# Prompt attention in one decoder layer: probabilities turned and multiplied with the values one or two steps behind their logits

## The reference

```python
logits = einsum(q, k) * 64 ** -0.5          # two maps m = 0, 1 per head, width 64 each
bias   = rel_bias[t5_bucket(q_pos - k_pos)] # depends on the distance alone
p      = softmax(where(dist >= 0, logits + bias, -1e30))
attn   = p[:, :, 0] - lam * p[:, :, 1]
out    = einsum(attn, v)                    # then RMSNorm over the 128 columns of a head
```

## Time and profile before

| what | value |
|---|---|
| median of three runs | 1768.83 us (1766.42 to 1769.52) |
| the profiled execution's own time | 1766.95 us |
| its span | 1765.1 us |
| TensorE busy in the span | 1553.6 us |
| mean granted clock of TensorE | 0.94 |
| the prompt's attention | about 484 to 908 us of the span |

### The profile page before, as it was taken

The page is one execution under the profiler, slowest core; times in us unless marked ns, Lnnn a source line. Parts: engine busy times, 40 slices in busy tenths (PEclk is TensorE's granted clock), DMA queues, the critical chain, the costliest instruction groups (busy, mean ns, idle before and its releaser), DMA issues. The chain is left out here.

```text
span 1765.1 us, 22053 instructions
## 1 busy us (share of the span) xinstructions
PE 1553.6 (88%) x7497; PEld 1061.8 (60%) x7498; DVE 707.0 (40%) x1465; ACT 461.4 (26%) x1040; POOL 232.3 (13%) x417
## 2 busy tenths in 40 slices
PE   5999889977499899898879999999889937999996
PEld 3555556555356565555558888888768733444442
DVE  4356877666524444454542221233242251212220
ACT  2223333322123333333432121122132210111110
POOL 1000101010122221222210000000000001222221
PEclk8999999988789998999979999999989968999998
DMA  7000300000030202000034766523253383988973
GB/s 246 16 1 17 116 2 26 1 2 25 26 114 1 62 1 62 1 26 1 1 121 135 249 205 204 168 72 110 84 158 108 108 288 105 317 247 231 297 215 48
DMA packets 119369, 186.03 MB, mean 105 GB/s; under 512 B 9507, under 2 KB 82262, under 8 KB 117222
## 3 DMA queue, kind: packets, MB, share of 16 engines
q1 hardware_dynamic: 107750, 134.41, 24.0%
q0 software_dynamic: 11520, 50.34, 9.8%
HBM read 154.38 MB, written 30.34 MB: 105 GB/s over the span
## 5 line engine op out<-in xcount | busy, mean ns | idle before, releaser
L964 PE MATMUL psum<-attention_part,kept 128*128 128x384 f32 (+1 forms) x576 | 201.0, 504 | 0.8 <-DVE attention_part L1197 0.7
L2158 PE MATMUL psum<-moe_part,kept 128*128 x384 | 172.4, 603 | 6.4 <-issue 4.9
L964 PEld LDWEIGHTS psum<-attention_part,kept 128*128 128x128 f32 (+1 forms) x576 | 108.0, 192 | 76.1 <-issue 16.5
L1430 PE MATMUL psum<-split 128*128 128x368 f32 x384 | 140.6, 366 | 2.5 <-DVE split L1576 2.5
L498 PE MATMUL psum<-kept,recurrence_part 128*128 128x368 f32 x384 | 124.4, 480 | 10.0 <-PEq L236 5.0
L1419 PE MATMUL psum<-kept,sample_part 128*128 128x368 f32 x384 | 131.8, 487 | 1.3 <-PEq L865 1.3
L503 PE MATMUL psum<-recurrence_part,kept 128*128 128x512 f32 (+1 forms) x288 | 126.5, 594 | 1.3 <-DVE kept L684 1.3
L1432 PE MATMUL psum<-split 128*128 128x368 f32 x384 | 127.3, 332 | 0.0
L1431 PE MATMUL psum<-split 128*128 128x368 f32 x384 | 127.0, 331 | 0.0
L2158 PEld LDWEIGHTS psum<-moe_part,kept 128*128 128x128 f32 x384 | 72.3, 193 | 89.7 <-issue 89.7
L518 PE MATMUL psum<-recurrence_part 128*128 128x128 f32 (+1 forms) x480 | 70.8, 308 | 48.9 <-DVE recurrence_part L767 39.4
(11 more groups left out here) (312 smaller groups left out, 2519.6 us busy)
## 6 DMA issues: line engine op xcount, KB each, us to landing
sample_part<-merge_gates POOLq DMA_DIRECT2D x16, 1024.0 KB
merge_part<-cache_kT SPq DMA_DIRECT2D x64, 256.0 KB, 3.3
merge_part<-cache_v SPq DMA_DIRECT2D x64, 256.0 KB, 3.0
moe_part<-w_gate SPq DMA_DIRECT2D x16, 1024.0 KB, 6.1
moe_part<-w_up SPq DMA_DIRECT2D x16, 1024.0 KB, 12.5
moe_part<-w_down SPq DMA_DIRECT2D x16, 1024.0 KB, 14.1
recurrence_part<-w_in SPq DMA_DIRECT2D x8, 1024.0 KB, 8.2
sample_part<-merge_out POOLq DMA_DIRECT2D x16, 512.0 KB, 6.5
```

Source lines behind the costliest of these rows:

```text
L964: mm = pe.matmul(bank_of(("z", h, i))[:ROWS[i], 0:384], K["xT"][:, k, cols(i)], Wb[h % 2][:, k, :], start=(k == 0), stop=(k == KC - 1))
L1430: pe.matmul(bank_of(u, 2 * j + 1), wh[w % 2][:, k, ch], xh[b][:, k, :], start=(k == 0), stop=False)
L2158: mm = pe.matmul(psum[:, 2 + par, :], XT[par][:, k, :], K["GU"][:, bass.ds(KC * b + k, 1), :], start=(k == 0), stop=(k == KC - 1))
```

## The change

The turned probabilities and their product with the values are put two steps behind the logits: slot s turns `Am` of step s - 2 and multiplies it; g of step s - 3 follows. There are 39 slots in place of 38. `Am` gets a second buffer, used by odd and even steps in turn, and `combine(s)` waits for the turning of step s - 2 in place of s - 1. `aT`, `Pm`, the banks and the place of z, L and x stay.

```diff
--- before.py
+++ after.py
@@ -844,17 +844,17 @@
     for n in range(1, AHEAD):
         zx += [make[n], place[n - 1]]
     slots = []
-    for s in range(STEPS + 2):
+    for s in range(STEPS + 3):
         slot = make[s + AHEAD:s + AHEAD + 1]
-        if 1 <= s <= STEPS:
-            slot += [("a", s - 1, g) for g in range(groups(s - 1))]
+        if 2 <= s <= STEPS + 1:
+            slot += [("a", s - 2, g) for g in range(groups(s - 2))]
         if s < STEPS:
             slot += [("L", s, 0), ("L", s, 1)] + ([("e", s, 0)] if s % NQ == NQ - 1 else [])
-        if 1 <= s <= STEPS:
-            slot += [("o", s - 1, 0)]
+        if 2 <= s <= STEPS + 1:
+            slot += [("o", s - 2, 0)]
         slot += place[s + AHEAD - 1:s + AHEAD]
-        if s >= 2:
-            slot += [("g", s - 2, 0)]
+        if s >= 3:
+            slot += [("g", s - 3, 0)]
         slots.append(slot)
     jobs = zx + [j for slot in slots for j in slot if j[0] != "L"]
     turn_of = {j: n for n, j in enumerate(jobs)}
@@ -883,7 +883,7 @@
         Bn = [sb(256) for _ in range(HEADS)]
         rel, rel31, relh, bucket, vecs = sb(HEADS), sb(HEADS), sb(HEADS, P), sb(ND), sb(HEADS, ND)
         Pm = sb(2, SEQ + META)
-        Am, aT = sb(SEQ + META), sb(NT, P)
+        Am, aT = sb(2, SEQ + META), sb(NT, P)
         nmax, sums, coef, ssq, rr, mt = sb(STEPS, 4), sb(STEPS, 4), sb(STEPS, 4), sb(STEPS), sb(STEPS, 2), sb(2, META)
         junk, og = sb(P), sb(2, P)
         block = st.enter_context(nc.Block())
@@ -1006,7 +1006,7 @@
                 bank_free(pe, ("a", s, g))
                 for n in range(4 * g, min(4 * g + 4, i + 1)):
                     w = META if n == i else P
-                    mm = pe.transpose(bank_of(("a", s, g))[:w, P * (n % 4):P * (n % 4) + r], Am[:r, P * n:P * n + w], K["ident"][:r, :r])
+                    mm = pe.transpose(bank_of(("a", s, g))[:w, P * (n % 4):P * (n % 4) + r], Am[:r, s % 2, P * n:P * n + w], K["ident"][:r, :r])
                 mm.then_inc(a_turned, 1)
 
             def outputs(s):
@@ -1241,9 +1241,9 @@
                 dve.drain()
                 dve.tensor_scalar(coef[:r, s, 0:1], sums[:r, s, 0:1], coef[:r, s, 3:4], K["lam"][:r, 3:4], ALU.mult, ALU.mult)
                 dve.drain()
-                if s:
-                    dve.wait_ge(a_turned, a_index[("a", s - 1, groups(s - 1) - 1)] + 1)
-                dve.scalar_tensor_tensor(Am[:r, 0:n], Pm[:r, 1, 0:n], coef[:r, s, 0:1], Pm[:r, 0, 0:n],
+                if s >= 2:
+                    dve.wait_ge(a_turned, a_index[("a", s - 2, groups(s - 2) - 1)] + 1)
+                dve.scalar_tensor_tensor(Am[:r, s % 2, 0:n], Pm[:r, 1, 0:n], coef[:r, s, 0:1], Pm[:r, 0, 0:n],
                                          ALU.mult, ALU.add).then_inc(a_done, 1)
 
             def scale_out(s):
@@ -1284,8 +1284,8 @@
                         normalise(a, b)
                 if s < STEPS:
                     combine(s)
-                if 1 <= s <= STEPS:
-                    scale_out(s - 1)
+                if 2 <= s <= STEPS + 1:
+                    scale_out(s - 2)
 
 
 def load_merge_weights(e, A, K, n):
```

## The result

The changed kernel takes 1.0055 times the time of the kernel before (95% interval 1.0037 to 1.0073): 1779.61 us as the median of 11 runs against 1769.69. By the ratio that is about 9.7 us more. The forecast was 3.9 us more, so the direction held and the size did not. The profiled execution has a span of 1775.1 us at a mean clock of 0.937.

The account below looks back on a forecast made before the run. It took TensorE as the bound, with 45 us idle in the attention. Terms -2.6 - 1.8 - 3.9 + 6.9 + 5.3 = +3.9 us on the 1768.8 median gave 1772.7; own range 1770 to 1776, chance 0.55.

Parts of the forecast that it names:

- The start: Slot 1: turning and o of step 0 leave it, 2.6 us gained, and the next z regains 1.8 us of clock.
- 0 as the other end: Slot 1's next z: 1.8 us gained at full clock, or 0 if the clock is not regained.
- Inside the heads: Tiles 2 to 8 of each head: shorter turning ahead of L, 3.9 us gained over all slots.
- the 0.12 and 0.2: Inside a head: 0.12 us gained per slot by one block less turned, 0.2 us in each tile-5 slot.
- These slots are held by the chain L, maxima, L1197: Tiles 2 to 8: the chain, then x or g, sets slot length, so only the shorter turning gains, 0.12 us a block.
- The changes of head: First two slots of heads 2 to 4: tile-0 gains 1.3 us, tile-1 is 3.6 longer; 2.3 net, three times, +6.9.
- D: Rival: the clock falls at each change of head, slower still; +11.1 us, 1779.9; chance 0.12.
- The drain: Slots 34 to 36: o(34) waits for VectorE's copy and delays o(35); costs 5.3 us.
- rival B: Drain: its o run at full clock, 3.4 us come back, no change; +0.5 us, 1769.3; chance 0.25.
- The prediction's C: Slots 34 to 36: waits for `combine` go, L(34) begins straight behind the turning; -7.7 us, 1761.1; chance 0.08.
- the interior would give nothing: Inside the heads: by the skill's rule a second `Am` alone is the wrong buffer, no gain, where the forecast counts 3.9.

Follow-up runs that it names:

- e_heads: Against the kernel before: two steps behind in the middle only, step 0 and steps 28 to 35 one step behind; ratio 1.0066.
- c_bank: Changed kernel with o(tile 7) and o(tile 8) of the first three heads in PSUM banks 1 and 3; ratio 0.9979 against the kernel before.
- c_fill: Changed kernel with two idle matmuls in the wait ahead of o(34); ratio 1.0035 against the kernel before.
- a_buffer: Kernel before with the second Am buffer alone, in the old order; ratio 1.0008 against the kernel before.
- e_start: Against the kernel before: step 0 alone two steps behind, all others one step behind; ratio 1.0006.
- e_drain: Against the kernel before: one step behind up to step 27, two steps behind from step 28; ratio 1.0030.
- b_between: Kernel before with VectorE's normalise between the two maxima, not behind both; ratio 0.9963 against the kernel before.
- c_between: Changed kernel with normalise between the two maxima; ratio 0.9959 against the kernel before.
- b_bank: Kernel before with o(tile 8) of the first three heads in PSUM bank 1; ratio 0.9963 against the kernel before.
- b_bank_between: b_bank with normalise between the two maxima; ratio 0.9931 against the kernel before.
- c_bank_between: c_bank with normalise between the two maxima; ratio 0.9920 against the kernel before.
- c_bank_between_fill: c_bank_between with the two idle matmuls ahead of o(34); ratio 0.9909 against the kernel before, 1752.46 us.

## Why the prediction came out wrong in size

The sum was +3.9 and the traces have +8.9. The terms that failed are the lower clock at the changes of head, which the forecast took as nothing more than before, and the lower clock of the logits in the drain.

*The start* held: -5.3 for -4.5. The z of slot 2 ran at full clock, which I had taken with 0 as the other end, and slot 2 itself was shorter.

*Inside the heads* -2.4 came for the -3.0 of these slots. The tile-5 slot got shorter by 0.32 to 0.33 us in each of the four heads, which is the 0.12 and 0.2 that I gave it, and those of tiles 6 and 7 by 0.05 to 0.14. Tiles 3 and 4 didn't follow: from 0.45 us shorter to 0.19 longer. "These slots are held by the chain L, maxima, L1197" is wrong for tile 2 as well. In the second head it took 3.58 us from the turning to the next z (624.00 to 627.58) after and 3.53 before (623.08 to 626.61 in the trace of before), although a block less was turned; in the third head 3.44 and 3.91. What holds these short slots isn't settled.

*The changes of head*: forecast +6.9 (+6.2 as the stretches are cut), found +9.1. The waits came where they were put. At the first change the tile-0 slot without its slow z would be 9.8 us for 11.2, a gain of 1.4 where I had 1.3; the tile-1 slot without its slow o is 11.6 for 8.56, 3.0 for the 3.6. That is a cost of 1.6 where I had 2.3, and 1.5 and 1.4 at the other two. The step that failed is the one by which I gave D 0.12 and put its cost into the sum as nothing: that the clock would fall no more than before, because the idle time in these slots would be no more than before. It was no more, and yet the clock fell at all three changes, twice each: o(tile 6) 0.9 to 1.0 us, z 2.0 to 2.1 and o(tile 8) 1.4 to 1.6 over their times at full clock, about 4.5 a head, 13.7 in all. The measured +9.7 is nearer to D's +11.1 than to the forecast. D's own account was short too. It found 3.6 us of such falls in the trace of before, which has about 1.8, 5.5 and 1.2, 8.5 in all. So the clock cost 5.2 us here that the sum lacked, and the waits came 2.3 us cheaper than forecast, which hid half of it: that the total of this term is off by only 2.9 is luck. Part of the 5.2 is the draw of one trace of before; by the means of several traces (e_heads, above) it is 3.6. The second change, where the trace of before had its worst, shows nothing at all (0.0).

c_bank shows what decides for o(tile 8): its place behind a wait. Why o(tile 6) and its z are slow isn't settled. In the four traces of the two-step order that keep the 2.8 to 2.9 us wait ahead of that o (changed, e_heads, c_bank, c_fill), the z behind it took 7.3 us or more in 12 places of 12; in the old order, behind the same wait, in 8 of 15. No kernel here changes only that.

*The drain*: forecast +5.3 (+5.2 as cut), found +7.6. The waits were those named: the turning's second groups for L1254 at slots 34 and 35, o(34) for VectorE's copy behind `combine(35)`, o(35) behind `scale_out(34)`. One was not named, the turning of step 34 for the exponentials (2.8 us at L1009, the bank of e); o(34) would have waited for its copy all the same. The term that was mis-sized is the clock's: L(35) took 5.24 us in place of 4.20, which made `combine(35)` later, L(34) took 5.2 in place of 4.75, and o(35) 4.47 in place of 4.06. Together these are 1.9 of the 2.4 us. I had kept the lower clock for the o and forgot it for L. The prediction's rival B, the two o of the drain at full clock, was worth the 3.4 us I gave it (c_fill: 3.4), but doesn't come by itself.

*The prediction's C* is excluded: TensorE waited 2.47 us for L1254 at 876.61, where L would else have begun.

The Trainium skill's rule on a repeated bubble (Perfetto Trace Analysis, Optimization Strategy, which is where it stands, and not in the section that the prediction names) is that it can mean too little SBUF or PSUM for the next tile. The runs agree as to PSUM: a second buffer in SBUF changed nothing (a_buffer, 1.0008), and two more places in PSUM took off 13 us (c_bank). What I drew from it, that the interior would give nothing, didn't come: it gave 2.4 us. The Trainium skill's other rule (TensorE: Matmul & The Clock Gate, A second HAM failure mode: psum-queue depth-cycling) is that short stops between groups that cycle through PSUM banks make the clock swing between its two levels. That is what I underrated; c_bank and c_fill agree with it.

## What to carry to other kernels

Before work is put further behind its producer, list what each moved job waits for besides that producer. Here the bank four places ahead was the real bound, the deeper order costs 9.7 us with the old rotation and gains 3.7 with two more banks, and the old order gains 6.5 with one. An extra step of lag also has to be drained, and in the drain there is nothing left to cover the chain; where a wait of the length seen here is certain, what stands behind it should be priced at TensorE's lower clock (o(tile 8) ran slow in 22 places of 24), the logits too. And before falls of the clock are put down to an order, they must be counted in more than one trace of the old order.

## What the runs showed of the hardware

The same 18 entries of o(tile 8) stand at three changes of head in all 14 kernels, behind waits of different length:

| kernels | wait ahead, us | o(tile 8) took, us |
|---|---|---|
| before, a_buffer, e_start, e_drain, b_between | 1.8 | 3.2 to 4.1 in 14 places, 2.46 in one |
| changed, e_heads, c_fill | 1.6 to 1.8 | 3.4 to 4.1 in 8 places, 2.46 in one |
| c_between | 1.2 | 2.46 to 2.47 in 3 places |
| b_bank, b_bank_between | 0.6 to 0.8 | 2.44 in 6 places |
| c_bank, c_bank_between, c_bank_between_fill | none | 2.44 in 9 places |

So a wait of 1.6 to 1.8 us cost 0.4 to 1.0 times its own length again, in 22 places of 24, and one of 1.2 us or less cost nothing more, in 18 of 18. Two idle matmuls in a wait of 2.9 us brought the granted clock of the next stretch from 0.50 to 0.92. And two profiles of the same order (before and a_buffer) differ by 3 us in the attention (424.5 and 427.6), with the slow z and o at other places.
